# A two-layer mLSTM/SSD trunk on one core: decay distances from plain fp32 tiles, built ahead, and another order in the mixer's first group

## The chip, the cores and the metric

The kernel runs on one core of a Trainium2 chip. The metric is the time of one execution on the device in microseconds (us), as the median over several runs. PE is TensorE (PEld its weight loads), DVE is VectorE, ACT is ScalarE, POOL is GpSimd and SP is SyncE, which issues the weight transfers.

## What is computed

Two layers (DEPTH 2) on 256 tokens (SEQ) of width 1024, all in fp32. Each layer is a half-step SwiGLU FFN (hidden 2816), the mixer, a second half-step FFN and a gated per-layer embedding. The mixer is what matters here: one projection feeds an mLSTM with 4 heads and a Mamba-2 SSD with 32 heads in 4 groups. Both work in chunks of 128 tokens, so there are NC = 2 chunks.

```
proj = rmsnorm(h) @ w_in            # q, k, v, o_pre, i_pre, f_pre, z, xbc, dt_raw, gate_pre
dt   = softplus(dt_raw + dt_bias);  dA = dt * a_neg;  acs = cumsum(dA) in a chunk
decay[t,s] = exp(acs[t] - acs[s]) for s <= t, else 0        # per head
y_intra = (C_t . B_s) * decay[t,s] @ (x * dt)
y_inter = (C_t . state at the chunk's start) * exp(acs[t])  # only chunk 1 has a state
ha = mlstm(q, k, v, i, f);  yb = rmsnorm((y_intra + y_inter + x*d_skip) * silu(z))
h  = h + (sigmoid(g_a) * (ha @ w_a) + sigmoid(g_b) * (yb @ w_b)) @ w_out
```

The "distances" of the title are the sums acs[t] - acs[s], one 128x128 tile per head and chunk.

## The kernel before

**Split products.** A large product runs as three matmuls in fp32r, a reduced form of fp32: each fp32 operand is split in a high part and a rest (w_hi and w_lo, u_hi and u_lo), and hi·hi, lo·hi and hi·lo are added up in a bank of PSUM. Weights pass through a ring of three slots. SP loads w_raw, ACT copies it to w_hi (L483), DVE subtracts for w_lo (L768), and PE takes it. The sizes of one slot are 1024 rows by 256 columns, and one slot is a **unit**: 48 matmuls of 256 columns.

**Mixer.** A layer's mixer has four groups (body(0, True), then a loop over the other three). A group has nine units in the order BC (B and C of the SSD), QK, X01 and X23 (its x), V, Z0, Z1, O and GA. Their results go in turn to banks 0, 1 and 2 (unit p to bank p % 3), from which DVE reads them (evac, L968). Between the units stand the small products of the group, in plain fp32 or fp32r, in banks 3 to 7. Each engine's order is written out by hand, and semaphores tie the engines together: step(p) in ACT and DVE prepares the weights of unit p+2.

**Distances before.** The sum from s to t is a product with a triangular matrix of ones: segments (L1452 to L1466) multiplies tri_gt_r with R, where R[s',t] is dA[s'] for s' <= t. The work goes by quarters b of a group's 8 heads, in each chunk c. POOL builds R for two heads twice, from dA_hi and dA_lo (L426), into two buffers in turn, PE makes two matmuls of 256 columns of them, and after every quarter POOL may refill its buffer (seg_done, r_built). In chunk 1 PE also multiplies R with ones_r, which gives acs[t] itself, into banks 4 and 5. ACT takes the exp of a half (four heads) from the banks (L586 for the tiles, L594 for acs[t] into cs). The one bank of a distance is 4 + 2c + half.

**First group.** It also prepares the gates for all groups. small (L1416) projects 40 columns, softplus_gates on DVE makes dA (L912) and its two parts (L916, L918). gates (L1429 to L1433) multiplies dA for w_end and transposes the mLSTM's gate inputs to 4 rows, gate_rows on DVE (L924 to L946) runs the running sums and maxima over them and ends with M4 (L946), and gates_back (L1439) turns them back into columns (tokc, tok_ready). scores (L1481, L1482) needs M4.

**Last part of a group.** chunk heads of the mLSTM (L1519 to L1521), transposes of x (L1527), memory read (L1532), state (L1537), outputs in two parts (L1547, L1549), and the transposes of the normalised mLSTM rows (L1554). After the groups come four gate units (K_GB, banks q % 3), a column sum with its row scale rB (L703 on ACT), and a merge loop that starts in bank 0.

## Time and profile before

| | us |
|---|---|
| median of 3 runs | 1681.77 |
| lowest and highest run | 1680.89, 1685.76 |
| the profiled execution | 1680.02 |
| its span, first to last instruction | 1678.3 |
| PE busy | 1612.6 (96%) |
| DVE busy | 1050.1 (63%) |
| ACT busy | 729.3 (43%) |
| POOL busy | 264.3 (16%) |

The span is what the views of the trace measure, and the profiled execution's own time is 1.72 us above it. Matmuls are pipelined: one counts as busy for 0.28 us while the next starts 0.12 us after it, so the time that a matmul takes from PE is read from start to start. An idle time in the views is what stands between the end of one instruction and the start of the next on an engine, with the instruction that ended it.

### The profile page before, as it was taken

How to read it: one execution, taken by the hardware profiler on the slowest of the kernel's cores; microseconds unless marked ns; L12 is line 12 of the kernel's file. 1: busy time of each engine (PE TensorE's matmuls, PEld its weight loads, DVE VectorE, ACT ScalarE, POOL GpSimd, SP SyncE). 2: the span in 40 equal slices, each digit the busy share in tenths (PEclk: the TensorE clock that was granted, in tenths of full speed). 3: DMA queues.
4: the chain of work that ended last, by engine and by line, in shares of the span. 5: the costliest groups of instructions: out<-in, count | busy, mean ns of one | idle time of the engine just before them, and what ended most of it. 6: DMA issues, size and time to landing. Idle time of an engine off the chain costs nothing.

```text
span 1678.3 us, 24971 instructions
## 1 busy us (share of the span) xinstructions
PE 1612.6 (96%) x9888; PEld 1422.0 (85%) x9888; DVE 1050.1 (63%) x1288; ACT 729.3 (43%) x880; POOL 264.3 (16%) x272
## 2 busy tenths in 40 slices
PE   7999989999999999999999999899999999999997
PEld 5888788998999978888778888798999999788885
DVE  5544587777886645454665455877787765454445
ACT  5444434344345435343554444344344443544444
POOL 0000024455430000000000000355435300000000
PEclk9999989999999999999999999899999999999999
DMA  7555534454544555555555554254453455465551
GB/s 240 194 176 196 153 105 125 123 149 127 152 148 161 169 178 201 184 187 179 165 187 177 189 186 138 89 156 121 150 150 100 150 186 189 156 203 179 196 175 63
DMA packets 245236, 270.85 MB, mean 161 GB/s; under 512 B 12504, under 2 KB 226360, under 8 KB 245176
## 3 DMA queue, kind: packets, MB, share of 16 engines
q1 hardware_dynamic: 239472, 266.90, 49.5%
q10 hardware_dynamic: 5704, 3.13, 0.7%
q8 instruction: 40, 0.66, 0.2%
q14 instruction: 20, 0.16, 0.0%
HBM read 268.94 MB, written 1.05 MB: 161 GB/s over the span
## 4 chain that ended last, share of the span: by engine, by line
PE 83%; DVE 6%; issue 5%; POOL 3%; ACT 2%; DMA 0%; POOLq 0%; DVEq 0%; SPq 0%; ACTq 0%
PE bank L1291 26%; PE bank L1317 16%; PE bank L1319 16%; PE bank L1318 16%; DVE w_lo L768 2%; POOL R L426 2%; PE bank L1359 1%; PE bank L1465 1%; PE bank L1303 1%; PE bank L1304 1%; PE bank L1305 1%; PE bank L1635 1%; PE bank L1312 1%; PE bank L1547 1%; ACT w_hi L483 1%
## 5 line engine op out<-in xcount | busy, mean ns | idle before, releaser
L768 DVE TENSOR_TENSOR w_lo<-w_raw,w_hi 128x2048 fp32r<-128x2048 f32 x252 | 590.6, 2345 | 306.4 <-ACT w_hi L483 306.2
L483 ACT ACTIVATE w_hi<-w_raw 128x2048 fp32r<-128x2048 f32 x252 | 481.6, 1913 | 232.2 <-PE bank L1319 119.9
L1291 PE MATMUL bank<-u_hi,w_hi 128*128 128x256 f32 x1152 | 336.0, 292 | 2.5 <-DVE u_lo L803 2.5
L1291 PE MATMUL bank<-u_lo,w_hi 128*128 128x256 f32 x1152 | 331.0, 287 | 0.0
L1291 PE MATMUL bank<-u_hi,w_lo 128*128 128x256 f32 x1152 | 330.8, 287 | 0.0
L1291 PEld LDWEIGHTS bank<-u_hi,w_hi 128*128 128x128 f32 x1152 | 226.4, 197 | 7.4 <-issue 6.3
L1291 PEld LDWEIGHTS bank<-u_lo,w_hi 128*128 128x128 f32 x1152 | 226.5, 197 | 0.1
L1291 PEld LDWEIGHTS bank<-u_hi,w_lo 128*128 128x128 f32 x1152 | 226.2, 196 | 0.0
L398 POOL TENSOR_TENSOR rms<-var,m_half 128x2 f32<-128x2 f32 x11 | 7.7, 698 | 1084.3 <-DVE var L796 1071.1
L1317 PE MATMUL bank<-w_hi,u_hi 128*128 128x512 f32 x416 | 166.3, 400 | 5.9 <-DVE u_lo L803 4.3
L1317 PE MATMUL bank<-w_hi,ha_hi 128*128 128x512 f32 x416 | 164.9, 396 | 3.5 <-DVE w_lo L768 3.5
L1319 PE MATMUL bank<-w_hi,u_lo 128*128 128x512 f32 x416 | 162.9, 392 | 0.0
L1318 PE MATMUL bank<-w_lo,u_hi 128*128 128x512 f32 x416 | 162.5, 391 | 0.0
L1319 PE MATMUL bank<-w_hi,ha_lo 128*128 128x512 f32 x416 | 162.4, 390 | 0.0
L1318 PE MATMUL bank<-w_lo,ha_hi 128*128 128x512 f32 x416 | 162.0, 389 | 0.0
L1317 PE MATMUL bank<-w_hi,h_hi 128*128 128x512 f32 x352 | 140.0, 398 | 0.4
L1319 PE MATMUL bank<-w_hi,h_lo 128*128 128x512 f32 x352 | 139.2, 396 | 0.0
L1318 PE MATMUL bank<-w_lo,h_hi 128*128 128x512 f32 x352 | 139.1, 395 | 0.0
L537 ACT ACTIVATE h_hi<-bank 128x512 fp32r<-128x512 f32 x44 | 26.3, 598 | 165.4 <-PE bank L1359 165.4
L1317 PEld LDWEIGHTS bank<-w_hi,u_hi 128*128 128x128 f32 x416 | 78.5, 189 | 22.5 <-DVE w_lo L768 6.4
L1317 PEld LDWEIGHTS bank<-w_hi,ha_hi 128*128 128x128 f32 x416 | 78.1, 188 | 21.0 <-DVE w_lo L768 5.3
L1319 PEld LDWEIGHTS bank<-w_hi,u_lo 128*128 128x128 f32 x416 | 78.4, 188 | 16.8
(259 smaller groups left out, 2579.9 us busy)
## 6 DMA issues: line engine op xcount, KB each, us to landing
w_raw<-in_w_ffn_dram SPq DMA_DIRECT2D x264, 512.0 KB, 4.3
w_raw<-in_w_in_dram SPq DMA_DIRECT2D x160, 512.0 KB, 4.6
w_raw<-in_w_branch_b_dram SPq DMA_DIRECT2D x32, 512.0 KB, 3.9
w_raw<-in_w_branch_a_dram SPq DMA_DIRECT2D x16, 512.0 KB, 4.0
w_raw<-in_w_out_dram SPq DMA_DIRECT2D x16, 512.0 KB, 4.2
w_raw<-in_w_ple_gate_dram SPq DMA_DIRECT2D x16, 512.0 KB, 4.2
y_feat<-in_w_ple_dram ACTq DMA_DIRECT2D x2, 1024.0 KB, 4.9
h<-in_x_dram SPq DMA_DIRECT2D x2, 512.0 KB, 4.9
```

What stands on the lines that cost most here:

```text
L426: i = g_.tensor_tensor(R[:, b % 2, q, :, :], tri_le[:, :].unsqueeze(1).broadcast_to([P, 2, P]), part[:, c, bass.ds(g * EH + 2 * b, 2)].bit ...
L483: a_.activation(whi[slot][:, :, :], raw[slot][:, :, :], ACT.Copy).then_inc(sem["w_hi"], 1)
L537: a_.activation(h1_hi[b][:, :, :], two(6 - 2 * b), ACT.Copy).then_inc(sem["h1_hi_ready"], 1)
L768: v_.tensor_tensor(wlo[slot][:, :, :], raw[slot][:, :, :], whi[slot][:, :, :].bitcast(F32), ALU.subtract).then_inc(sem["w_lo"], 1)
L1291: i = mm(o, w[slot][:, k, cs], x[:, k, :], start=(k + q == 0 and not seeded), stop=(k == KD - 1 and q == 2 and not seeded), skip_group_che ...
L1303: mm(o, xh[:, k, cs], whi[slot][:, k, :], start=(k == 0), stop=False)
L1304: mm(o, xh[:, k, cs], wlo[slot][:, k, :], start=False, stop=False)
L1305: i = mm(o, xl[:, k, cs], whi[slot][:, k, :], start=False, stop=(k == KD - 1))
L1312: ins = nc.tensor.transpose(bank[b][:, chunk(t)], h[:, c, (4 * q + t) * P:(4 * q + t + 1) * P], ident[:, :])
L1317: mm(o, xh, wh, start=start, stop=False, skip_group_check=True)
L1318: mm(o, xh, wl, start=False, stop=False, skip_group_check=True)
L1319: return mm(o, xl, wh, start=False, stop=stop, skip_group_check=True)
```

## The change

Distances: R is now plain fp32 and holds four heads for one chunk (128x512). POOL builds it with one multiplication from dA instead of four of 256 columns. The two R tiles lie in the storage of xwe and zth, which the group uses later. The products use tri_gt and ones in plain fp32, one matmul of 512 columns per tile: four tiles a group for the distances (seg_done counts to 6 a group instead of 8), and two (from_start, banks 6 and 7) for acs[t], read from the same R. The two tiles of chunk 0 are built by POOL in the group before (at its end, ahead of the ysum addition). dA_hi and dA_lo are gone.

Order: in the later groups each distance tile stands half a unit or more away from the one before, and from_start lies in the middle of V. In the first group gates moves from the last quarter of X23 to ahead of X23, gates_back and scores move into the middle of V, from_start lies in Z0, and the chunk's last products move one unit back. cb no longer waits for the exp of acs[t]. M4 has 128 rows, cleared by POOL once a layer. The gate units after the groups use banks 0, 1, 0, 2, and the merge loop waits for their evacuation instead of for rB. chunk_heads, inputs_transposed, memory_read, state and outputs are the same code as before, now as functions (their waits are the same but that the transposes also wait for the exp of acs[t], since both use banks 6 and 7).

```diff
+    GATE_BANK = (0, 1, 0, 2)
...
-        M4 = sb("M4", [MH, MH, S])
+        M4 = sb("M4", [P, MH, S])
...
-        R, _ = at("R", [P, 2, 2, 2, P], F32R, a)
...
+        R = (xwe[:, :].rearrange("p (e t) -> p e t", e=4),
+             zth[:, :, :].rearrange("p a b -> p (a b)").rearrange("p (e t) -> p e t", e=4))
...
+            def distances_of(g, c, half):
+                g_.tensor_tensor(R[half][:, :, :], tri_le[:, :].unsqueeze(1).broadcast_to([P, 4, P]),
+                                 dA[:, c, bass.ds(g * EH + 4 * half, 4)].unsqueeze(2).broadcast_to([P, 4, P]),
+                                 ALU.mult).then_inc(sem["r_built"], 1)
...
+                def token_columns():
+                    pool.wait_ge(sem["tok_ready"], lay * 2 + 2)
+                    g_.tensor_copy(gtk[:, :].unsqueeze(2), tokc[:, :, bass.ds(g, 1)]).then_inc(sem["gtk_ready"], 1)
+                if first:
+                    pool.wait_ge(sem["dA_ready"], lay + 1)
+                    for half in range(2):
+                        distances_of(g, 0, half)
+                else:
+                    token_columns()
+                for half in range(2):
+                    pool.wait_ge(sem["seg_done"], G * 6 + (half + 1))
+                    distances_of(g, 1, half)
+                if first:
+                    token_columns()
...
+                if not last:
+                    pool.wait_ge(sem["yi_done"], G + 1)
+                    pool.wait_ge(sem["zth_ready"], G * 2 + 2)
+                    for half in range(2):
+                        distances_of(g + 1, 0, half)
...
+                g_.memset(M4[:, :, :], 0.0).then_inc(sem["m4_clear"], 1)
+                group(lay, 0, True, False)
+                with nc.gpsimd.Fori(1, NG - 1) as g:
+                    group(lay, g, False, False)
+                group(lay, NG - 1, False, True)
...
-                            act.wait_ge(sem["seg_done"], G * 8 + 10)
-                            a_.activation(cs[:, 4 * b:4 * b + 4, :], bank[4 + b][:, :].rearrange("p (e t) -> p e t", e=4),
+                            act.wait_ge(sem["seg_done"], G * 6 + (5 + b))
+                            a_.activation(cs[:, 4 * b:4 * b + 4, :], bank[6 + b][:, :].rearrange("p (e t) -> p e t", e=4),
...
                     step(2)
-                    if not first:
-                        decay(0)
-                    step(3)
                     if first:
+                        step(3)
                         act.wait_ge(sem["cum_done"], lay + 1)
                         a_.activation(w_end[:, :], bank[7][:, 0:SH], ACT.Exp).then_inc(sem["cum_exp"], 1)
+                        step(4)
                         decay(0)
                         act.wait_ge(sem["row_back"], lay + 1)
...
                         tanh_conv(1, xcv[:, 0:2, :])
+                        score_exp()
+                        step(5)
+                        decay(1)
+                        transposed_copies()
+                        decay_from_start()
+                        tanh_conv(2, xcv[:, 2:4, :])
                     else:
+                        decay(0)
+                        step(3)
                         tanh_conv(1, xcv[:, 0:2, :])
                         score_exp()
                         decay(1)
+                        step(4)
                         decay_from_start()
-                    step(4)
-                    if first:
-                        score_exp()
-                    tanh_conv(2, xcv[:, 2:4, :])
-                    if first:
-                        decay(1)
-                        decay_from_start()
...
-                    step(5)
+                        tanh_conv(2, xcv[:, 2:4, :])
+                        transposed_copies()
+                        step(5)
...
-                ch.add(v_.tensor_copy(dA_hi[:, :, :], dA[:, :, :]))
-                ch.wait()
-                v_.tensor_tensor(dA_lo[:, :, :], dA[:, :, :], dA_hi[:, :, :].bitcast(F32), ALU.subtract)\
-                    .then_inc(sem["dA_ready"], 1)
+                v_.scalar_tensor_tensor(out=dA[:, :, :], in0=spx[:, :, 4:36], scalar=-1.0,
+                                        in1=e_a[:, :].unsqueeze(1).broadcast_to([P, NC, SH]),
+                                        op0=ALU.mult, op1=ALU.mult).then_inc(sem["dA_ready"], 1)
...
                     conv(1, 1, (2, 3), xcv[:, 0:2, :])
                     silu(1, xcv[:, 0:2, :])
-                    if not first:
+                    if first:
+                        distances()
+                    else:
                         weigh_scores()
-                    else:
-                        distances()
                     evac(X23, xin[:, 0, :, 3:])
+                    if first:
+                        values()
+                        step(4)
+                        weigh_scores()
+                        mask_cb()
                     taken(X23)
                     conv(2, 0, (4, 5), xcv[:, 2:4, :])
...
+                    if not first:
+                        values()
                     silu(2, xcv[:, 2:4, :])
-                    if first:
-                        weigh_scores()
-                    mask_cb()
-                    step(4)
+                    if not first:
+                        mask_cb()
+                        step(4)
                     dve.wait_ge(sem["ysum_ready"], G + 1)
                     evac(Z0, zs[:, 0:2, :])
                     step(5)
...
+                    if not first:
+                        weighted_inputs()
                     dve.wait_ge(sem["z_tanh"], G * 2 + 1)
                     v_.scalar_tensor_tensor(out=zs[:, 0:2, :], in0=zth[:, :, :], scalar=1.0, in1=zs[:, 0:2, :],
                                             op0=ALU.add, op1=ALU.mult).then_inc(sem["zth_ready"], 1)
                     step(6)
                     evac(Z1, zs[:, 2:4, :])
+                    if first:
+                        weighted_inputs()
...
-                        for b in (2 * half, 2 * half + 1):
-                            pe.wait_ge(sem["r_built"], G * 8 + (4 * c + b + 1))
-                            todo = [(4 + 2 * c + half, tri_gt_r)]
-                            if c == 1:
-                                pe.wait_ge(sem["exp_done"], G * 4 + (half + 1))
-                                todo.append((4 + half, ones_r))
-                            for bk, w in todo:
-                                for q in range(2):
-                                    i = mm(bank[bk][:, (b % 2) * S:(b % 2 + 1) * S], w[:, :],
-                                           R[:, b % 2, q, :, :], start=(q == 0), stop=(q == 1))
-                            i.then_inc(sem["seg_done"], 1)
+                        pe.wait_ge(sem["r_built"], G * 4 + (2 * c + half + 1))
+                        mm(bank[4 + 2 * c + half][:, :], tri_gt[:, :], R[half][:, :, :], start=True, stop=True)\
+                            .then_inc(sem["seg_done"], 1)
+                    def from_start():
+                        for half in range(2):
+                            pe.wait_ge(sem["exp_done"], G * 4 + (3 + half))
+                            mm(bank[6 + half][:, :], ones[:, :], R[half][:, :, :], start=True, stop=True)\
+                                .then_inc(sem["seg_done"], 1)
                     def cb():
                         pe.wait_ge(sem["cv_ready"], G * 3 + 1)
-                        pe.wait_ge(sem["acs_exp"], G * 2 + 2)
+                        pe.wait_ge(sem["exp_done"], G * 4 + 2)
...
                         unit(QK, lambda *a: feat(*a, between=lambda: norm_rows(lay, 1)))
                         small_back(lay)
                         unit(X01, feat)
-                        unit(X23, lambda *a: feat(*a, between=lambda: gates(lay)))
+                        gates(lay)
+                        unit(X23, feat)
                         segments(0, 0)
-                        gates_back(lay)
                         segments(0, 1)
-                        scores()
+                        def rows_and_scores():
+                            gates_back(lay)
+                            scores()
+                        unit(V, lambda *a: tok(*a, between=rows_and_scores))
                         pe.wait_ge(sem["tok_ready"], lay * 2 + 2)
-                        unit(V, lambda *a: tok(*a, between=lambda: segments(1, 0)))
+                        segments(1, 0)
                         segments(1, 1)
                         cb()
+                        unit(Z0, lambda *a: feat(*a, between=from_start))
+                        chunk_heads()
+                        unit(Z1, feat)
+                        inputs_transposed()
+                        memory_read()
+                        unit(O, feat)
+                        state()
+                        outputs(0)
+                        outputs(1).then_inc(sem["y_done"], 1)
                     else:
                         unit(BC, feat)
-                        unit(QK, feat)
-                        segments(0, 0)
-                        unit(X01, lambda *a: feat(*a, between=lambda: segments(0, 1)))
-                        segments(1, 0)
+                        unit(QK, lambda *a: feat(*a, between=lambda: segments(0, 0)))
+                        segments(0, 1)
+                        unit(X01, lambda *a: feat(*a, between=lambda: segments(1, 0)))
+                        segments(1, 1)
                         evac(QK)
                         scores()
-                        unit(X23, lambda *a: feat(*a, between=lambda: segments(1, 1)))
-                        unit(V, tok)
+                        unit(X23, feat)
+                        unit(V, lambda *a: tok(*a, between=from_start))
                         cb()
-                    unit(Z0, feat)
...
+                        unit(Z0, feat)
+                        chunk_heads()
+                        inputs_transposed()
+                        unit(Z1, feat)
+                        memory_read()
+                        state()
+                        outputs(0)
+                        unit(O, feat)
+                        outputs(1).then_inc(sem["y_done"], 1)
...
-                    feat((K_GB + q) % RING, q % 3, u_hi, u_lo)
+                    pe.wait_ge(sem["evac"], lay * NE + (NG * GU + (q + 1 if q != 2 else RING + 1)))
+                    feat((K_GB + q) % RING, GATE_BANK[q], u_hi, u_lo)
                     if q == 0:
...
-                    pe.wait_ge(sem["yB_ready"], lay + 1)
+                    pe.wait_ge(sem["evac"], lay * NE + (NG * GU + RING + 3))
```

**PE, first group, around the gates.** w_hi_54 is the slot of X01, w_hi_52 that of X23. Before:

```order
L1291 MATMUL bank<-u_hi,w_hi_52 128x256
L1291 MATMUL bank<-u_lo,w_hi_52 128x256
L1291 MATMUL bank<-u_hi,w_lo_55 128x256
L1429 MATMUL bank<-dA,tri_gt 128x32
L1432 MATMUL bank<-ident,pre 4x128
L1433 MATMUL bank<-ident,spx 4x128
L1432 MATMUL bank<-ident,pre 4x128
L1433 MATMUL bank<-ident,spx 4x128
L1291 MATMUL bank<-u_hi,w_hi_52 128x256
L1291 MATMUL bank<-u_lo,w_hi_52 128x256
```

After:

```order
L1316 MATMUL bank<-u_hi,w_hi_54 128x256
L1316 MATMUL bank<-u_lo,w_hi_54 128x256
L1316 MATMUL bank<-u_hi,w_lo_57 128x256
L1454 MATMUL bank<-dA,tri_gt 128x32
L1457 MATMUL bank<-ident,pre 4x128
L1458 MATMUL bank<-ident,spx 4x128
L1457 MATMUL bank<-ident,pre 4x128
L1458 MATMUL bank<-ident,spx 4x128
L1316 MATMUL bank<-u_hi,w_hi_52 128x256
L1316 MATMUL bank<-u_lo,w_hi_52 128x256
```

The gates stood inside X23 and stand ahead of it now, 36 matmuls earlier.

**PE, later groups, from X01 to the scores.** REGISTER_ALU and ISA rows are waits' bookkeeping. Before:

```order
L1465 MATMUL bank<-R,tri_gt_r 128x256 x2
L1465 MATMUL bank<-R,ones_r 128x256 x2
L1458 REGISTER_ALU
L1465 MATMUL bank<-R,tri_gt_r 128x256 x2
L1465 MATMUL bank<-R,ones_r 128x256 x2
L1452 REGISTER_ALU
L1481 MATMUL bank<-qT,kT 128x128 x2
L1482 ISA
L1482 MATMUL bank<-M_89,ones 128x256
```

After:

```order
L1316 MATMUL bank<-u_hi,w_hi_54 128x256
L1316 MATMUL bank<-u_lo,w_hi_54 128x256
L1316 MATMUL bank<-u_hi,w_lo_57 128x256
L1481 REGISTER_ALU
L1482 MATMUL bank<-zth,tri_gt 128x512
L1477 REGISTER_ALU
L1503 MATMUL bank<-qT,kT 128x128 x2
L1504 ISA
L1504 MATMUL bank<-M_82,ones 128x256
```

Eight matmuls in two waited-for steps (half 0 of chunk 1) stood here; one plain fp32 tile (half 1 of chunk 1) does now, and half 0 lies in X01.

**POOL, end of a group.** Before:

```order
L442 TENSOR_TENSOR seg<-seg,cbm 128x1024
L445 REGISTER_ALU
L446 TENSOR_TENSOR cs<-cs,bcv 128x1024
L398 TENSOR_TENSOR hrms<-hvar,m_half 128x2
L451 TENSOR_TENSOR ysum<-ysum,zs 128x1024
```

After:

```order
L444 TENSOR_TENSOR seg<-seg,cbm 128x1024
L447 REGISTER_ALU
L448 TENSOR_TENSOR cs<-cs,bcv 128x1024
L397 TENSOR_TENSOR hrms<-hvar,m_half 128x2
L404 ISA
L404 TENSOR_TENSOR xwe<-tri_le,dA 128x512
L404 ISA
L404 TENSOR_TENSOR zth<-tri_le,dA 128x512
L458 TENSOR_TENSOR ysum<-ysum,zs 128x1024
```

The next group's two tiles of chunk 0 now stand between hrms and ysum.

## Rows read from the trace of the kernel before

**Rows 1.** The page: busy us, share of the span and instructions of each engine.

```profile
PE 1612.6 (96%) x9888; PEld 1422.0 (85%) x9888; DVE 1050.1 (63%) x1288; ACT 729.3 (43%) x880; POOL 264.3 (16%) x272
```

**Rows 2.** Waits of PE in the whole span: us in total, times, longest.

```profile
PE bank L1465 <- POOL R L426: 14.0, 12, 2.0
PE bank L1439 <- DVE M L946: 8.3, 2, 4.2
...
PE bank L1465 <- ACT seg L586: 3.8, 6, 1.7
PE bank L1474 <- ACT cs L594: 3.7, 2, 2.0
PE bank L1291 <- ACT rB L703: 3.1, 2, 1.6
```

**Rows 3.** Stretches of PE: length, busy (instructions), granted clock, DMA share, GB/s.

```profile
227.76:289.71 61.95, 54.03 (x414) 0.89 0.37 103
1052.22:1114.63 62.41, 54.60 (x413) 0.89 0.36 109
289.71:494.00 204.29, 197.64 (x1618) 0.97 0.49 138
1114.63:1321.72 207.09, 199.61 (x1617) 0.97 0.44 137
428.30:494.00 65.70, 64.01 (x542) 1.00 0.50 142
```

**Rows 4.** Timeline of PE, a quarter pair's distances: start, us, engine, line, operation.

```profile
450.44 0.64 PE L1465 MATMUL bank<-R,tri_gt_r 128*128 128x256 f32 x4
450.91 0.27 PE L1291 MATMUL bank<-u_hi,w_hi 128*128 128x256 f32 x1
```

**Rows 5.** Timeline of PE, plain fp32 products and the unit behind them.

```profile
349.05 0.59 PE L1532 MATMUL bank<-cst,qT 128*128 128x257 f32 x2
349.48 1.02 PE L1537 MATMUL bank<-xwe,btok 128*128 128x512 f32 x2
350.43 1.09 PE L1547 MATMUL bank<-seg,xw 128*64 128x128 f32 x16
351.46 0.39 PE L1291 MATMUL bank<-u_hi,w_hi 128*128 128x256 f32 x1
351.68 0.28 PE L1291 MATMUL bank<-u_lo,w_hi 128*128 128x256 f32 x1
```

**Rows 6.** Timeline of PE, first group of layer 0: X01, gates, gates_back.

```profile
227.76 0.39 PE L1291 MATMUL bank<-u_hi,w_hi 128*128 128x256 f32 x1
...
238.09 0.41 PE L1429 MATMUL bank<-dA,tri_gt 128*128 128x32 f32 x2
...
247.41 2.72 PE L1439 MATMUL bank<-ident,r_x 4*128 4x4 f32 x12 [4.08 <-DVE M L946]
```

**Rows 7.** Timeline of DVE, first group of layer 0: dA, and the gate rows.

```profile
237.32 0.23 DVE L912 SCALAR_TENSOR_TENSOR dA<-spx,e_a 128x64 f32<-128x64 f32 x1
...
246.15 1.20 DVE L946 TENSOR_TENSOR M<-r_m,ident 4x1024 f32<-4x1024 f32 x1
```

**Rows 8.** Timeline of all engines, the same group's mLSTM norm.

```profile
283.85 0.42 ACT L660 ACTIVATE pm<-num 128x256 f32<-128x256 f32 x1 [1.22 <-DVE num L1090]
...
286.36 0.62 DVE L1110 TENSOR_SCALAR num<-num,hsc 128x256 f32<-128x256 f32 x2
```

**Rows 9.** Timeline of all engines, second group: X23's start, the chain beside it.

```profile
320.05 0.58 PE L1291 MATMUL bank<-u_hi,w_hi 128*128 128x256 f32 x1
...
320.23 0.61 DVE L1009 TENSOR_SCALAR pm<-bank,gtk 128x128 f32<-128x128 f32 x2 [3.35 <-PE bank L1482]
...
328.05 1.07 ACT L586 ACTIVATE seg<-bank 128x512 f32<-128x512 f32 x2
```

**Rows 10.** Timeline of POOL, second group, building R.

```profile
314.69 2.66 POOL L426 TENSOR_TENSOR R<-tri_le,dA_lo 128x256 fp32r<-128x256 f32 x1
317.31 0.61 POOL L426 TENSOR_TENSOR R<-tri_le,dA_hi 128x256 fp32r<-128x256 f32 x1
```

210 lines of the change are left out of this document (96 added, 114 removed).

## The prediction

> **What bounds the kernel now.** The page comes first: PE is busy 96% of the span, DVE 63%, and no other engine is near that [rows 1]. So the time is PE's work plus PE's idle time, and next one reads who PE waits for. The waits view of PE over the span names five causes that touch the lines of this change: R from POOL 14.0 us, M4 from DVE 8.3, the exp of seg 3.8, the exp of cs 3.7 and rB 3.1, together 32.9 us, all in the mixer [rows 2]. The third view cuts PE's time into stretches and gives the granted clock of each. Both first groups (from the start of X01 to the start of GA) have a clock of 0.89 and all later groups of a layer together 0.97, but the last group of layer 0 alone 1.00: 65.70 us with 64.01 busy [rows 3]. That last row is the measure for all: a later group is 64.0 us of work at the full level of 2.4 GHz. What stands above it in the others is idle time and time at the half level of 1.2 GHz, in which a unit's matmuls need twice the time. The six later groups take 204.29 + 207.09 = 411.4 us, 27.4 above 6 x 64.0 [rows 3]; 14.1 of these are idle (411.38 less 197.64 and 199.61 busy), 13.3 the clock.
>
> **The change, part by part.**
>
> *Plain fp32 tiles, PE's price.* Before, a tile of four heads is four fp32r matmuls of 256 columns, 0.47 us from start to start [rows 4]; six tiles a group are 2.8 us. No row has a plain fp32 matmul with R, so its price is bounded. A plain product of 257 columns holds PE 0.43 us (349.05 to 349.48), which is 0.86 for 512; the product of 512 columns takes 0.95 until the next starts [rows 5]. I take 0.86, since the tiles are of the same shape as the first scaled up and have no narrow output behind them, and keep 0.95 as the upper end. Behind plain products the first matmul of a unit holds 0.22 instead of 0.12 (351.46 to 351.68) [rows 5]; I put as much on the way in, 0.2 for each place where plain work newly interrupts a unit. A later group has four such places (in QK, behind it, in X01, in V; the fourth tile joins the scores, which are plain already): 6 x 0.86 + 0.8 - 2.8 = 3.2, taken as 3.1; the ends are 2.4 (no cost of switching) and 3.7. A first group has one new place: +2.6. So PE gets 6 x 3.1 + 2 x 2.6 = 23.8 us more work. This is the debit side, and it is most of what the waits offer.
>
> The Trainium skill speaks against this part: "FP8 and Floating Point Precision", section TensorE Precision Notes, says that true fp32 needs four passes through the array. Four passes of 512 columns at 2.4 GHz would be 0.853 us, an estimate from that page, and by it the tiles alone cost 48 x (0.853 - 0.47) = 18.4 us.
>
> *R built by one multiplication, chunk 0 a group ahead.* POOL takes 0.61 us for 256 columns undisturbed and 2.66 when it falls together with a DVE operation [rows 10], so a tile of 512 costs 1.2 us, or about 3.3 when disturbed. Half of each pair is now built while the mLSTM norm or output work runs, 18 us before PE needs it; the other half is built after the first tiles (three quarters through QK, and behind it) and needed three quarters through X01, 5.8 us or 48 x 0.12 later, and behind X01. Both fit, even disturbed. The eight matmuls that waited in two steps on the exp of seg and on a refilled R are gone, since the ones product is a step of its own in V. So the 14.0 and the 3.8 us go. POOL's two builds ahead stand before ysum, which waits for ACT's square anyway; they may push one w_lo of DVE by 2 us, and the unit it serves starts 10 us later.
>
> *What is late next in a later group.* from_start, in the middle of V, waits for the exp of chunk 1's seg. The row of before gives both sides from X23's start at 320.05: PE needs a unit (5.76) and half of V (2.88), 8.64 us; DVE's distances start 0.18 behind it, and the first of ACT's two exps starts at 328.05 and ends about 0.55 later, at 8.55 [rows 9]. The slack is nil. I take 0.2 us a group, ends 0 and 1.0. A later group is then 64.0 + 3.1 + 0.2 = 67.3 us at full clock, six are 403.8, against 411.4: **-7.6 us**. With no idle time over 1 us I expect no half clock there: the one later group that kept 1.00 had a single idle time of 1.69 [rows 3], and the R waits elsewhere reach 2.0 [rows 2].
>
> *First group.* Idle before is 61.95 - 54.03 = 7.9 us [rows 3], 4.08 of it at gates_back [rows 6]. Gone with the new order: gates_back stands half of V after the tiles, at about 249, and DVE's gate rows end at 247.35 [rows 7]; the two R waits (POOL starts on dA and has all of X23) and the cs wait at cb. New: gates stands ahead of X23. X01 starts at 227.76 and needs 5.8 us, so PE is there at 233.6; before it came at 238.09 [rows 6]. But dA, which gates multiplies, is only ready at 237.55 [rows 7]. dA_hi and dA_lo come behind dA, so their loss does not bring it forward. That is **4.0 us idle**, at a place that had none. Everything behind it on PE, X23 first, waits too. Second, state now comes one unit later but the last products follow at once: ACT squares the mLSTM rows only behind the copy of the state, and from that square's start to the end of num on DVE it is 283.85 to 286.98, 3.1 us [rows 8], plus 0.6 for the copy; both parts of outputs fill 2.9 us of it. 0.9 us idle. Clock: before, 0.11 x 61.95 is 6.8 us lost, that is 13.6 us at half, 4.1 of them idle, so 4.8 us of real loss. After, one idle time of 4.0 instead of four; I take half the time at half clock, a loss of 3.0, ends 1.5 and 6.8. Sum: +2.6 work, -7.9 + 4.9 idle, -4.8 + 3.0 clock = -2.2 each, **-4.4 us**.
>
> *Merge.* Bank 0 is free earlier, since the last gate unit writes bank 2, so PE need not wait for rB: **-3.1 us** [rows 2]. DVE alone needs rB, a unit and two more later. *Small.* M4's clearing (one POOL memset a layer of 1024 columns, some 1 us) falls ahead of the group's constants while DVE still works on the row scale; 0, at worst 1 us a layer. M4's product keeps its columns: 0.
>
> **Sum.** -7.6 - 4.4 - 3.1 = -15.1 us. On the profiled execution, 1680.02, that is 1664.9. The median of the runs lies 1.75 above that execution: **1667 us** against 1681.77, 0.9% less.
>
> **The rivals.**
>
> 1. *No new stall at the gates or no drop behind it.* If dA came earlier than 237.55, 4.0 + 3.0 would go twice: 1653. I see no reason in the rows for dA to move; only the clock may stay up, 6 us: 1661.
>
> 2. *The clock stays as it was.* The plain tiles do not mend the half level: 13.3 us in the later groups and 3.8 more in the first ones come back, -15.1 + 17.1 = +2: 1684, no change to be measured. For it speaks that a 4.0 us gap is in each first group as before; against it that the later groups have no gap of that kind left.
>
> 3. *Slower: from_start becomes the new wait.* Its slack is nil [rows 9]. If DVE's chain ahead of it slips, by one collision with POOL (2.66 against 0.61, 2 us [rows 10]), PE idles 2 us in V and falls to half for some 3.5 us, 1.7 lost: 3.7 x 6 = 22 us, and the result is 1689. It decides the sign from 15.1 / 6 = 2.5 us a group. Against it: in that stretch POOL has nothing queued between the R tiles and pm, which comes behind the exp.
>
> 4. *A part only.* The fp32 tiles cost their upper end (3.7) and from_start 1.0: +1.4 x 6 = 8 us: 1675.
>
> **Chances and range.** A difference of 0.3% (5 us) is about what a measurement of this kernel can tell from none. Forecast (1661 to 1671) 0.53; rival 1 0.12; rival 4 0.17; rival 2 0.10; rival 3 0.08. The range leaves out rival 3, most of rival 2 and the far part of rival 1: 1658 to 1679. Faster by over 0.3% (below 1676.7): 0.53 + 0.12 + most of rival 4 = 0.79; within: the rest of 4 and rival 2, 0.13; slower (above 1686.8) 0.08.
>
> **What would show it.** In the profile after, the waits view should have no R line from POOL beyond 1 us in total, no M4 wait, no rB wait, and a new wait of PE for dA, twice, 4.0 us each. The four-heads tile should hold PE 0.86 to 0.95 us. Each later group should be 67 to 68 us with a clock of 1.00, each first group about 59.8 from X01 to GA. A wait for seg at the ones product above 0.5 us a group speaks for rival 3, a clock under 0.98 in later groups for rival 2. The forecast is wrong if the stall at the gates is not there, if a plain tile costs over 1.1 us, or if idle times come up at places that the rows of before don't show, for instance weights (w_lo) in the first group, where DVE's order is rearranged.

## The result: 36.6 us faster, more than twice the forecast

| | before | after |
|---|---|---|
| median of 4 runs, us | 1681.67 | 1645.11 |
| lowest and highest | 1680.89, 1685.76 | 1644.43, 1645.88 |
| span of the profiled execution | 1678.3 | 1644.1 |

The ratio is 0.9772 (95% interval 0.9755 to 0.9788). The forecast was 1667 with a range of 1658 to 1679; the time lies 13 us below its lower end. The sign was right, the size was not.

The page after: PE is busy for 11.4 us less than in [rows 1] (the time at half clock counts as busy too), although the plain fp32 tiles were to cost it 23.8 more.

```profile
PE 1601.2 (97%) x9792; PEld 1399.9 (85%) x9792; DVE 1047.4 (64%) x1282; ACT 730.1 (44%) x880; POOL 205.4 (12%) x178
```

The waits of PE after (us in total, times, longest). None of the five of [rows 2] is left. dA, num and cst are new; the first two are nearly what the prediction said, twice 4.0 and twice 0.9. This view lists no wait for seg at from_start; a small one hides there all the same (see "M4 with 4 rows again").

```profile
PE bank L1454 <- DVE dA L931: 7.6, 2, 3.8
...
PE bank L1605 <- DVE num L1138: 1.7, 2, 0.9
...
PE bank L1527 <- ACT cst L667: 0.5, 2, 0.2
```

Stretches of PE after (length, busy, granted clock, DMA share, GB/s). The first four answer to [rows 3]: the two first groups, then the later groups of each layer. The last two are the end of layer 0's groups up to the merge loop, and what follows up to the end of the second FFN (merge, output projection, FFN), which the change leaves alone but for the merge loop's first wait.

```profile
226.05:284.58 58.53, 53.61 (x402) 0.94 0.41 112
1036.64:1093.96 57.32, 52.40 (x401) 0.97 0.38 111
284.58:482.14 197.56, 197.56 (x1581) 1.00 0.51 145
1093.96:1291.54 197.58, 197.58 (x1582) 1.00 0.47 144
482.14:513.10 30.96, 30.96 (x255) 1.00 0.38 122
...
513.10:816.30 303.20, 301.34 (x1631) 1.00 0.56 183
```

The same untouched stretch in the kernel before took 2.2 us more, with no other idle time and no other clock:

```profile
526.76:832.16 305.40, 303.53 (x1628) 1.00 0.54 180
```

The later groups have no idle time in this view and the full clock: 65.85 us each. Set beside the forecast, in us of the span (1678.3 to 1644.1):

| stretch | forecast | measured |
|---|---|---|
| six later groups | -7.6 | -16.2 |
| two first groups | -4.4 | -8.5 |
| to the merge loop, both layers | -3.1 | -3.6 |
| stages that the change leaves alone | 0 | -5.6 |
| the stretch ahead of X01, both layers | 0 | -0.3 |
| sum | -15.1 | -34.2 |

The last row but one is the clock ahead of the mixer: layer 0 has no half clock there after (-2.1 and +0.4), layer 1 has one (+1.4). No run ties it to the change.

### The profile page after: what moved, and what is told of

Read it like the earlier page. It is cut to its first block, busy times and chain, and to the rows that moved or that the text cites. A ratio compares the mean times of both kernels' runs of the same rounds, so it can differ in the third digit from the quotient of the medians.

```text
span 1644.1 us, 24426 instructions
## 1 busy us (share of the span) xinstructions
PE 1601.2 (97%) x9792; PEld 1399.9 (85%) x9792; DVE 1047.4 (64%) x1282; ACT 730.1 (44%) x880; POOL 205.4 (12%) x178
## 4 chain that ended last, share of the span: by engine, by line
PE 90%; DVE 5%; ACT 2%; issue 2%; DMA 0%; POOL 0%; SPq 0%; POOLq 0%; DVEq 0%; ACTq 0%
PE bank L1316 31%; PE bank L1342 16%; PE bank L1343 16%; PE bank L1344 16%; PE bank L1482 1%; DVE w_lo L787 1%; PE bank L1384 1%; PE bank L1330 1%; PE bank L1329 1%; PE bank L1328 1%; PE bank L1686 1%; ACT w_hi L499 1%; DVE xcv L997 1%; PE bank L1544 1%; PE bank L1488 1%
## 5 line engine op out<-in xcount | busy, mean ns | idle before, releaser
L1316 PE MATMUL bank<-u_hi,w_hi 128*128 128x256 f32 x1152 | 341.7, 297 | 2.5 <-DVE u_lo L822 2.5
L1316 PEld LDWEIGHTS bank<-u_hi,w_hi 128*128 128x128 f32 x1152 | 223.1, 194 | 9.3 <-issue 7.8
```

The source lines that it names most:

```text
L1316: i = mm(o, w[slot][:, k, cs], x[:, k, :], start=(k + q == 0 and not seeded), stop=(k == KD - 1 and q == 2 and not seeded), skip_group_che ...
```

## The experiments

The ratio in each compares with runs of the kernel before on the same chip, whose median there was 1681.8 to 1683.7. Line numbers are those of each kernel's own code.

### Where the operands lie: the stages that were not touched

The gain of 5.6 us in untouched stages needed a cause first. From start to start the merge matmuls with yb took 116.7 ns before and 113.5 after (mean of 752), the FFN matmuls with h1 233.1 and 229.0 (1030); those with u and ha did not move. yb and h1 are exactly the tiles that lie in the shared stage storage, and this begins 2400 bytes lower after the change, since tri_gt_r, ones_r, dA_hi, dA_lo and three sp tiles left the room below it.

```diff
+        top[0] += 32
         base = top[0]
         a = base
```

> The changed kernel with 32 bytes left free in front of all tiles that share the stage storage (h1_hi, h1_lo, yb_hi, yb_lo among them); nothing else is changed. In the changed kernel that storage begins 2400 bytes lower than before, at a multiple of 64 bytes instead of a multiple of 32 alone; here it begins at a multiple of 32 alone again, at nearly the same place. Theory alignment: this sets the spacing of the matmuls that read these tiles; the merge matmuls with yb go from 113.5 ns back to 116.7 and the FFN matmuls with h1 from 229.0 to 233.1, and the kernel takes about 5.2 us more (2.2 + 2.2 + 1.2 less 0.4, the gains in the stages that the change does not touch): 1650. Rival distance: what counts is the place 2400 bytes lower, or it is something else than the place: spacings stay at 113.5 and 229.0 and the time at 1645.

> The kernel before with the same 32 bytes, so that its stage storage begins at a multiple of 64 bytes, 2432 bytes above that of the changed kernel. Theory alignment: spacings fall from 116.7 to 113.5 ns (yb) and from 233.1 to 229.0 (h1), and the time falls by about 5.2 us: 1676.5. Rival distance: nothing moves, 1681.7.

Measured: e1 1652.75 us (ratio 0.9818, 0.9797 to 0.9840), yb 118.3 ns, h1 233.2. e2 1683.49 us (ratio 1.000, 0.9987 to 1.0013), yb 117.8, h1 233.4. Thirty-two bytes cost the changed kernel some 7 us, so the place is the cause. But e2's storage begins at a multiple of 64 and gained nothing: the theory of alignment fell. One loop of the merge, 96 matmuls with yb, in the kernel after, in e1 and in e2:

```profile
535.85:546.93 11.08, 11.08 (x99) 1.00 0.58 189
```

```profile
536.93:548.47 11.54, 11.54 (x98) 1.00 0.57 184
```

```profile
552.25:563.74 11.49, 11.49 (x99) 1.00 0.56 185
```

The next run puts the storage of the kernel before at the very byte where the changed kernel has it:

```diff
-        tri_gt_r = sb("tri_gt_r", [P, P], F32R)
-        ones_r = sb("ones_r", [P, P], F32R)
...
-        top_all = max(a, a2, a3, a4, a5)
+        a6 = max(a, a2, a3, a4, a5)
+        tri_gt_r, a6 = at("tri_gt_r", [P, P], F32R, a6)
...
+        top_all = a6
```

> The kernel before with tri_gt_r, ones_r, sp_a, sp_b, sp_c, dA_hi and dA_lo (2400 bytes a partition) moved behind everything else, so that the shared stage storage begins at the very byte where it begins in the changed kernel; nothing else is changed. Theory placement: the changed kernel's gain in stages that it does not touch comes from that place alone. Shifting by 32 bytes took 7 us from the changed kernel and gave the kernel before nothing, so it is the exact place and not its alignment alone: h1 matmuls go from 233.1 to 229.0 ns, yb from 116.7 to 113.5, time -5.2 us (2.2 + 2.2 + 1.2 - 0.4). Rival: the spacings come with the new code in another way: no change.

Measured: 1676.12 us, ratio 0.9955 (0.9937 to 0.9973), 5.7 us less than the median of the kernel before beside it (1681.82; the interval allows 4.5 to 10.6). yb 113.5, h1 229.0, to the tenth what the changed kernel has. So the 5.6 us that the forecast lacked come from the place.

What in the address counts? Three kernels put five operands at other distances from the weight slots; the lines shown are those of the second for u and yb:

```diff
+        def skip(off, residue):
+            while (off - origin) % 512 != residue:
+                off += 32
+            return off
+
+        origin = top[0]
         raw = [sb(f"w_raw{i}", [P, KD, NP]) for i in range(RING)]
...
+        top[0] = skip(top[0], 192)
         u_hi = sb("u_hi", [P, KD, S], F32R)
...
-        a2 = base
+        a2 = skip(base, 0)
```

> The changed kernel with five operands at other places, all by the distance of their first byte from that of the weight slots, modulo 512: u 64 (0 in both kernels), ha 128 (0), yb 256 (192 in the changed kernel), h1 buffer 0 256 and buffer 1 320 (192); the computation is the same. So far, for products whose moving operand has 256 columns, that distance and the spacing were: 0 (ha) 120.1 ns, 32 (yb, before) 116.7, 64 (yb) 117.8, 192 (yb, after) 113.5, 224 (yb) 118.3. Theory distance modulo 512: the spacing follows that number whichever tile it is, so u at 64 falls from 120 to 117.8, and that alone is 3456 x 2.3 ns = 8 us of the kernel. Rival: each tile has its own spacing by its absolute place or its role: u stays at 120.

> The same with u 192, ha 256, yb 0, h1 buffer 0 at 0 and buffer 1 at 128. Theory distance modulo 512: u at 192 takes the 113.5 ns of yb, 3456 matmuls x 6.6 ns = 23 us less, its products of 512 columns go from 227.6 to 229.0 (3 us more), and yb at 0 takes the 120.1 of ha (768 x 6.6 = 5 us more), h1 at 0 the 227.6 of u: about 1630. Rival (own spacing of each tile): u stays at 120 and the time within 5 us of 1645.

> The same with u 320, ha 384, yb 128, h1 buffer 0 at 384 and buffer 1 at 448. No distance among these has been measured. Theory distance modulo 512: what ha shows at 128 in the first of these kernels, yb shows here. Rival: they differ by over 1 ns.

Measured: e9 1655.25 us (one run), e10 1639.96 (ratio 0.9743, 0.9718 to 0.9769), e11 1653.98 (one run). The mean spacings from start to start, each over several hundred matmuls, by the distance modulo 256:

| distance | moving operand, 256 columns | stationary operand, 512 columns moved |
|---|---|---|
| 0 | u 119.8, ha 119.6, ha 120.0, yb 119.9 | u 227.6, ha 227.7, h1 227.1 |
| 32 | yb 116.7 | h1 233.1 |
| 64 | yb 117.8, u 117.4, u 117.5 | h1 233.4, u 233.3, u 233.3 |
| 128 | ha 118.7, yb 118.6, ha 118.6 | ha 232.6, ha 232.8 |
| 192 | yb 113.5, u 114.9 | h1 229.1, u 229.1 |
| 224 | yb 118.3 | h1 233.2 |

Different tiles at the same distance agree within 0.6 ns, except u at 192, which has 1.4 more than yb. Places 256 apart agree too. So the theory of e9 holds for the spacings, with a period of 256, and the two roles of the table want different places: the moving operand 192, the stationary one under 512 columns 0. A third role does not follow the table's second column. In V, u is the stationary operand and 256 columns of weights are moved (some 350 matmuls): 119.8 ns at 0, 114.6 and 114.1 at 64 (e9, e11), 115.6 at 192 (e10). There 0 is the worst of the places tried. From GA to the quarter of QK, 132 matmuls with u, in the kernel after and in e10:

```profile
350.42:366.34 15.92, 15.92 (x136) 1.00 0.33 80
```

```profile
349.47:364.53 15.06, 15.06 (x135) 1.00 0.26 73
...
530.60:542.30 11.70, 11.70 (x100) 1.00 0.57 183
```

u won 0.86 us in this stretch, and yb, put at 0 (the second row), lost 0.62 a loop. e9 and e11 were slow because u and ha as stationary operands went from 227.6 to 233, and yb from 113.5 to 119.9 and 118.6. For e10's time 1630 was expected and 1640 came: u took 114.9 ns and not 113.5, 4.6 us over 3267 matmuls, and PE, now faster, waited longer, for seg at from_start above all (2.3 us in the waits view).

In all these kernels the weight slots stood still, so distance and plain address were the same thing. One more run moved everything, the slots too:

```diff
+        top[0] += 64
         raw = [sb(f"w_raw{i}", [P, KD, NP]) for i in range(RING)]
```

> The changed kernel with every tile 64 bytes higher, the weight slots among them; all distances between tiles stay. Theory distance: the spacing of two operands' products is set by where they lie to each other, so nothing moves: u 119.8 ns, yb 113.5, h1 229.1, time 1645. Rival, plain address modulo 256: yb takes what it had at the next place 64 bytes up (119.9), u what it had at 64 (117.4), and the stationary u of 512 columns goes from 227.6 to 233: u alone 8 us less, yb and the stationary operands some 5 and 12 us more, about 1655, as the kernel with u at 64 had (1655.3).

Measured: 1644.83 us (one run); u 119.8, yb 113.5, h1 229.1. Nothing moved:

```profile
349.40:365.32 15.92, 15.92 (x135) 1.00 0.31 81
534.81:545.89 11.08, 11.08 (x98) 1.00 0.57 189
```

So the plain address falls, and what counts is where an operand lies to something that moved with it. That this is the weight slots is likely, since each of these products reads one, but no run moved the slots alone. Whether the operand meets PE's own weight loads or the writes of ACT, DVE and the DMAs into the slots stays open too: no run separates them.

Does placement help a kernel whose mixer waits? The kernel before, with u at 192, yb and h1 at 192 and ha at 0, by moving small tiles only:

```diff
+        dcol = sb("dcol", [P, SI // P])
+        w_end = sb("w_end", [P, SH])
         u_hi = sb("u_hi", [P, KD, S], F32R)
...
+        gcb = sb("gcb", [P, 6])
+        gdk = sb("gdk", [P, 4])
         ha_hi = sb("ha_hi", [P, 2 * MH, S], F32R)
```

> The kernel before with small tiles moved to other places and nothing else: the 2400 bytes behind everything as in the run with the low base, dcol and w_end ahead of u_hi and gcb and gdk ahead of ha_hi, so that u lies 192 bytes from a multiple of 256 (from the weight slots), ha at 0, yb and h1 at 192. Theory: the gain of the place is independent of the change: 5.6 us as with the low base, and of u's 3200 matmuls x 4.9 ns = 16 us less 1155 x 1.5 ns = 1.7 the part that waits do not eat; in the changed kernel a later group gained 1.65, the stretch to the merge loop 1.56 a layer, so at least 6 x 1.65 + 2 x 1.56 = 13 less 1.7: 1682 - 5.6 - 11 = 1665. Rival: PE's waits in the mixer of before (R, M4, seg, cs) take it back: 1671 to 1676.

Measured: 1670.61 us, ratio 0.9935 (0.9921 to 0.9948): 11.4 us less, of which the low base gives 5.7. The rival holds, at the edge of its 1671 to 1676. The later groups took 205.18 and 203.67 us against 204.29 and 207.09 in [rows 3], with 9 us idle in each layer where there were 6.7 and 7.5: PE is faster in its units and waits longer for R, 19.4 us instead of 14.0.

```profile
287.83:493.01 205.18, 196.22 (x1617) 0.96 0.48 138
1111.44:1315.11 203.67, 194.66 (x1617) 0.97 0.46 139
```

```profile
PE bank L1466 <- POOL R L427: 19.4, 16, 2.3
```

### The price of a plain fp32 tile

```diff
+                        mm(bank[4 + 2 * c + half][:, :], tri_gt[:, :], R[half][:, :, :], start=True, stop=True)
                         mm(bank[4 + 2 * c + half][:, :], tri_gt[:, :], R[half][:, :, :], start=True, stop=True)\
                             .then_inc(sem["seg_done"], 1)
```

> The changed kernel with every distance tile of segments issued twice into the same bank: four plain fp32 matmuls of 512 columns more a group, 32 in all. Theory: the tile costs PE 0.86 us and interrupting a unit of fp32r matmuls costs nothing on top; a later group goes from 65.85 to 69.3 us (+3.4) and the kernel's six later groups take +20.6; in the first groups the four tiles stand in an engine order where PE waits anyway, +0 to +6.9 for both. 1666 to 1673. Rival (the prediction's price, with 0.2 for each place where plain work interrupts a unit inside the present group): a second copy behind the first costs 0.86 and the present tile 1.06, so that the group would have to show 0.2 more at the first copy than at the second. Second rival, the upper end of 0.95 a tile: 69.65 a later group.

Measured: 1671.02 us, ratio 0.9931 (0.9913 to 0.9949). The later groups of a layer take 207.93, 69.31 each, against 65.85. Four more tiles are 3.45 us, so 0.863 a tile.

```profile
285.91:493.84 207.93, 207.93 (x1606) 1.00 0.48 137
```

The timeline of the same kernel at the quarter of QK (start, us, engine, line, operation; x2 because one plain product of 512 columns is recorded as two matmuls), where L1482 is the first copy and L1483 the second:

```profile
301.70 0.28 PE L1316 MATMUL bank<-u_hi,w_lo 128*128 128x256 f32 x1
301.83 1.02 PE L1482 MATMUL bank<-xwe,tri_gt 128*128 128x512 f32 x2
302.69 1.02 PE L1483 MATMUL bank<-xwe,tri_gt 128*128 128x512 f32 x2
303.14 0.68 PE L1316 MATMUL bank<-u_hi,w_hi 128*128 128x256 f32 x1
303.66 0.28 PE L1316 MATMUL bank<-u_lo,w_hi 128*128 128x256 f32 x1
```

The copy behind the unit holds PE 0.86, and from the second copy to the unit's second matmul there are 0.97, which is 0.86 and the usual 0.12. Interrupting a unit with such a tile costs nothing. The theory holds; both rivals fall. The unit's first matmul behind a tile starts early and lasts long: its work has moved up into the tile's time and is not lost. Whether this is so for the 0.22 of [rows 5], which stands behind smaller products, no run separates. True fp32 as four passes of 512 columns at 2.4 GHz, an estimate of 0.853 us from the Trainium skill ("FP8 and Floating Point Precision", TensorE Precision Notes), agrees with the 0.863 measured.

### M4 with 4 rows again

```diff
-                        mm(bank[3][:, S:2 * S], ones[:, :], M4[:, bass.ds(g, 1), :].rearrange("p a b -> p (a b)"),
+                        mm(bank[3][:, S:2 * S], ones[0:MH, :], M4[0:MH, bass.ds(g, 1), :].rearrange("p a b -> p (a b)"),
```

> The changed kernel with M4's product on 4 rows again (ones and M4 cut to 4 partitions) instead of 128. Theory: a product with 4 rows among full ones costs PE 0.3 to 0.4 us more a group (1.39 us from the scores to the unit's second matmul before, 1.00 after), eight groups: +2.4 to +3.1 us, 1648. Rival: that difference came from elsewhere (the waited-for exp, fp32r products ahead of it): no change, 1645.

Measured: 1648.56 us, ratio 0.9791 (0.9769 to 0.9814). From the scores to the second matmul behind them 1.38 us instead of 1.00; a later group takes 66.04 instead of 65.85. So the 128 rows gave 0.38 us at the place but 0.19 in the length of a group, 1.1 us in six of them. The rest of the difference in time is mostly layer 1's first group, whose clock was lower (60.44 us at 0.92 against 57.32 at 0.97), so that the time hit its forecast in part by luck.

The other 0.19 stands at from_start. In the changed kernel its two products start 0.86 us apart in the first group, where seg is long ready, and 0.97 apart in a later group:

```profile
261.67 1.02 PE L1488 MATMUL bank<-xwe,ones 128*128 128x512 f32 x2
262.53 1.02 PE L1488 MATMUL bank<-zth,ones 128*128 128x512 f32 x2
...
386.53 1.13 PE L1488 MATMUL bank<-xwe,ones 128*128 128x512 f32 x2
387.50 1.02 PE L1488 MATMUL bank<-zth,ones 128*128 128x512 f32 x2
```

The first of them also starts 0.20 behind the unit's matmul and not 0.12. Together that is a wait for seg of 0.18 us in each of the six later groups, too short for the idle column, since a matmul counts as busy for 0.28. In e4 PE comes there 0.38 later, both steps are 0.12 and 0.86 in all later groups, and the wait is gone.

The scores and the unit behind them, in the kernel with M4 on 4 rows, and then in the changed kernel:

```profile
376.61 0.61 PE L1503 MATMUL bank<-qT,kT 128*128 128x128 f32 x4
377.14 0.69 PE L1504 MATMUL bank<-M,ones 4*128 x2
377.76 0.39 PE L1316 MATMUL bank<-u_hi,w_hi 128*128 128x256 f32 x1
377.99 0.28 PE L1316 MATMUL bank<-u_lo,w_hi 128*128 128x256 f32 x1
```

```profile
376.94 0.61 PE L1503 MATMUL bank<-qT,kT 128*128 128x128 f32 x4
...
377.94 0.28 PE L1316 MATMUL bank<-u_lo,w_hi 128*128 128x256 f32 x1
```

### The banks of the gate units alone

The kernel before with GATE_BANK (0, 1, 0, 2) and the merge loop's wait on the evacuation instead of rB.

> The kernel before with one part of the change alone: the four gate units use banks 0, 1, 0, 2 and the merge loop waits for their evacuation instead of for rB. Theory: the stretch from GA of the last group to the merge loop goes from 32.76 to 30.96 us in each layer as it did with the whole change, -3.6 us in all, 0.5 more than the wait of 3.1 that the prediction counted; everything else stays. Rival: the stretch became shorter with the rest of the change (the last group ends otherwise, POOL's ysum): -3.1 or less.

Measured: 1680.30 us, ratio 0.9986 (0.9976 to 0.9996). The stretch to the merge loop is 30.97 us in both layers, as expected and as with the whole change:

```profile
493.99:524.96 30.97, 30.97 (x255) 1.00 0.39 126
1323.05:1354.02 30.97, 30.97 (x255) 1.00 0.37 122
```

So -3.6 us there, 0.5 more than the wait of [rows 2]. In the whole time less of it is seen, since layer 1's first group took 64.10 us instead of 62.41, with a clock of 0.87.

### Building ahead, taken back

POOL builds the tiles of chunk 0 at the start of their own group:

```diff
-                if not last:
-                    pool.wait_ge(sem["yi_done"], G + 1)
-                    pool.wait_ge(sem["zth_ready"], G * 2 + 2)
-                    for half in range(2):
-                        distances_of(g + 1, 0, half)
...
                 else:
+                    for half in range(2):
+                        distances_of(g, 0, half)
                     token_columns()
```

> The changed kernel without the building ahead: POOL builds the two tiles of chunk 0 at the start of their own group, behind the group's constants, instead of at the end of the group before. Theory: it is the building ahead that lets the later groups run without idle time. In the second group POOL is through with the constants at 301.4 and PE is at the first tile at 300.5, so the tile comes at 302.4 undisturbed (1.04 us) or at 304.5 beside a DVE operation (3.1): 2 to 4 us idle a later group, and half clock behind it (1.5 to 3 more, as the later groups of the kernel before stand at 65.7, 68.5 or 70.0 us): 66.9 + 2 to 4 + 1.5 = 68 to 72 a group, 1658 to 1680. Rival: the four tiles instead of eight quarters and their spread are what counts, and the tile comes in time: 1645 to 1650.

Measured: 1647.04 us (one run), 1.9 more than the changed kernel. The rival holds. Only the second group of each layer is longer (67.4 against 65.9), PE waits 1.3 us for the tile there; in the third and fourth groups it comes in time.

```profile
PE bank L1478 <- POOL xwe L404: 2.6, 2, 1.3
```

The building ahead is worth 1.5 us in the second group of each layer, about 3 in all. The rest of the idle time went out of the later groups without it. That this is because a chunk needs two tiles instead of four refilled pairs, with half a unit or more of PE's work between two tiles, fits the rows but is not shown: no run takes the number and the order of the tiles apart.

### The first group: the stall at gates

The kernel with gates in X23 again, then the same with POOL's products kept away from a convolution, and last this edit without moving gates:

```diff
-                        gates(lay)
-                        unit(X23, feat)
+                        unit(X23, lambda *a: feat(*a, between=lambda: gates(lay)))
```

> The changed kernel with one move undone: in the first group gates stands after three quarters of X23 again instead of ahead of it. Theory: the two idle times of 3.8 us at gates and the half clock behind them come from that move alone. dA is ready at 235.8 in both; X23 would start at 232.1, so PE is at gates at 236.4 and does not wait. X23 then takes 5.8 us instead of 8.0 and PE is 6.0 us earlier in layer 0 (3.8 + 2.2) and 5.5 in layer 1 (3.8 + half of 3.4). Against it stands a new wait at gates_back in V: the gate rows end at about 244.1 as now, PE is there at 242.9: 1.2 us each. Together 9 us less: 1636. Rival: the gate rows are the true bound (DVE's chain after them sets what comes later, X01's evacuation and the first exps), so that waits of the same 3.8 us come up further on: 1642 to 1645.

Measured: 1647.19 us, ratio 0.9783 (0.9761 to 0.9804), nothing gained. The waits for dA are gone, and others stand in their place, these two the largest:

```profile
PE bank L1527 <- ACT cst L667: 4.3, 2, 2.2
...
PE bank L1464 <- DVE M L961: 3.0, 2, 1.5
```

The first groups are as long as with the stall (the rival), at a clock of 0.97:

```profile
226.20:285.45 59.25, 52.91 (x402) 0.97 0.41 113
1037.53:1095.30 57.77, 52.78 (x401) 0.97 0.38 110
```

cst is late because ACT waits for DVE's evacuation of Z0, and this stands behind the third convolution. In the changed kernel DVE's two rows of it take 2.82 and 6.69 us, while POOL multiplies seg:

```profile
258.83 2.82 DVE L994 TENSOR_SCALAR xcv<-xin,gcw,gcb 128x256 f32<-128x256 f32 x2
261.69 6.69 DVE L997 SCALAR_TENSOR_TENSOR xcv<-xin,gcw,xcv 128x256 f32<-128x256 f32 x6
```

```profile
259.00 4.87 POOL L444 TENSOR_TENSOR seg<-seg,cbm 128x1024 f32<-128x1024 f32 x2 [4.48 <-DVE cbm L1030]
264.27 2.51 POOL L448 TENSOR_TENSOR cs<-cs,bcv 128x1024 f32<-128x1024 f32 x1 [0.40 <-ACT cs L610]
```

```diff
+                if first:
+                    pool.wait_ge(sem["conv_done"], G * 3 + 3)
                 pool.wait_ge(sem["cbm_done"], G + 1)
```

> The changed kernel with gates back inside X23 and, in the first group alone, one wait more on POOL: its seg multiplications begin when DVE's third convolution is through. Theory from the run with gates in X23 alone, which took away both stalls at gates and gained nothing (1647.2): in the first group DVE is the bound, and its third convolution takes 9.7 us (2.8 + 6.9) instead of 3.4 because it stands beside POOL's two multiplications of 1024 columns; PE waits 1.1 us for xcv and 2.2 for cst behind it. With the two apart DVE is about 6 us earlier at the evacuation of Z0, these waits go, and the half clock after them: 3.3 to 5 us a layer, 1637 to 1641. Rival: POOL's products come too late then (m_ready, cs_ready) or DVE's next operations, the weights, take the collision instead: 1644 to 1648.

Measured: 1641.75 us, ratio 0.9760 (0.9744 to 0.9776). The convolution takes 3.5 us instead of 9.5, the waits for cst and xcv are gone (that for num grew from 0.9 to 1.7 a layer), and both first groups are 56.47:

```profile
257.78 0.73 DVE L996 TENSOR_SCALAR xcv<-xin,gcw,gcb 128x256 f32<-128x256 f32 x2
258.54 2.71 DVE L999 SCALAR_TENSOR_TENSOR xcv<-xin,gcw,xcv 128x256 f32<-128x256 f32 x6
```

In the changed kernel three of the convolution's eight instructions take 2.5 us where each takes 0.4 to 0.5 alone, and the first of the three ends at 261.65, 0.15 behind POOL's product. That fits what the Trainium skill says in "SBUF — State Buffer", section SBUF: two separate sides: DVE and GpSimd share a pair of ports that one of them holds for a whole instruction.

> The changed kernel with POOL's seg products behind the third convolution in the first group, and gates left ahead of X23 where the change put it. Theory: DVE is the bound of the first group once gates is there; the stall of 3.8 us at gates delays X23 but DVE's chain, which begins with dA, not: as with gates in X23 (1641.8), within 2 us. Rival (the prediction's step): now that the collision is gone, the stall at gates and the half clock behind it are on the path and cost 3 to 6 us a layer: 1648 or more.

Measured: 1644.33 us, ratio 0.9777 (0.9762 to 0.9792), between the two. From X01 to GA, in layer 0 and layer 1:

| | gates ahead of X23 | gates in X23 |
|---|---|---|
| POOL beside the convolution | 58.53, 57.32 | 59.25, 57.77 |
| POOL behind it | 58.14, 57.95 | 56.47, 56.47 |

As whole kernels the four took 1645.11 (nothing), 1647.19 (gates in X23), 1644.33 (POOL behind) and 1641.75 us (both). Neither edit alone gains clearly, both together do: 2.1 and 0.9 us in the groups, 3.4 in the median, with all of its runs below all runs of the changed kernel. Single cells of the table hold the clock of one execution: the upper left is at 0.94 and 0.97, the lower left at 0.94 twice, the right column at 0.97, and e4 and e12, which have this part as in the upper left, show 57.57 and 60.44, and 57.17 and 57.29. Two chains of nearly equal length end in this group, PE's with the stall at gates and DVE's with the convolution. The theory (stall hidden) and the rival (stall on the path) are each half right: the stall is as late as the thing that would come next.

### A version that beats both

gates in X23, POOL behind the convolution, u and yb at 192, ha and h1 at 0:

> The changed kernel with gates in X23, POOL's seg products behind the third convolution in the first group, and operands placed by what the runs showed (distance from the weight slots modulo 256): u 192 and yb 192, which are mostly the moving operand, ha 0 and h1 0, which are mostly the stationary one. Theory placement by residue: yb at 113.5 ns as in the changed kernel (119.9 at 0: 768 x 6.4 ns = 4.9 us less than the kernel with u 192, ha 256 and yb 0, which took 1640.0), h1 at 227.6 instead of 229.7 (2.2 us less), and 3.4 us less from the first groups, as that edit gave alone: 1640 - 4.9 - 2.2 - 3.4 = 1629.5. Rival: the terms don't add up, since PE comes faster to DVE's first group and waits there, 1633 or more.

Measured: 1629.69 us, ratio 0.9694 (0.9681 to 0.9707), 15.4 us less than the changed kernel and what the sum of single terms (1629.5) said. u 114.9 ns, yb 113.5, h1 227.1.

```profile
226.24:282.75 56.51, 51.77 (x402) 0.97 0.42 114
1027.54:1084.06 56.52, 50.16 (x402) 1.00 0.39 114
282.75:475.69 192.94, 191.81 (x1582) 1.00 0.52 149
```

The later groups are 64.3 and 64.5 us now. They idle for 1.1 us a layer: PE's units have become so fast that the wait for seg at from_start, 0.18 us a group in the changed kernel, shows in the waits view (seg, 2.3 us in all).

## Why the prediction was wrong, step by step

**The bound, the waits and what they leave: right.** PE was the bound. R, M4, seg, cs and rB left the waits view. The later groups kept the full clock, as forecast, here and in every kernel built on the changed one. Rival 2 did not come, nor rival 3: PE reaches from_start a little before seg is ready and waits 0.18 us in each later group, where the prediction took 0.2 from a slack of nil.

**PE's price of the tiles: the term that was mis-sized most.** The tile was put at 0.86 and measured 0.863 (e5). The step that failed is the 0.2 us for each of four places where plain work interrupts a unit: they are 0. M4's product was said to keep its price because it keeps its columns; on 128 rows it costs 0.38 us less (e4). And the fp32r work that went was 2.95 us in the last group of layer 0 (24 matmuls, start to start), not 2.8. So a later group got 6 x 0.863 - 2.95 - 0.38 = 1.85 us more work instead of 3.1.

The measured length agrees: 65.85 - 64.0 = 1.85. Two small waits cancel in it. The 64.0 of [rows 3] hold 0.15 us of waiting, since the group's idle time of 1.69 moved PE's next start by 1.84 (452.22 to 454.18 in the timeline of before, less the usual 0.12); and the changed kernel waits 0.18 at from_start. So the group was forecast at 67.3 and took 65.85, and six times 1.45 is the 8.6 that the later groups missed, up to rounding. The lower bound that the prediction wrote for this term (2.4, no cost of switching) was nearly the truth. The reading that failed was of [rows 5]: the longer gap behind plain products was taken for a price of every switch, though the row ahead of it has to be read with it. The timeline of the changed kernel shows the whole of it, 0.98 us from the tile to the unit's second matmul:

```profile
300.48 1.02 PE L1482 MATMUL bank<-xwe,tri_gt 128*128 128x512 f32 x2
300.94 0.68 PE L1316 MATMUL bank<-u_hi,w_hi 128*128 128x256 f32 x1
301.46 0.28 PE L1316 MATMUL bank<-u_lo,w_hi 128*128 128x256 f32 x1
```

**First groups: the idle times right, the rest too high.** Idle after is 58.53 - 53.61 = 4.92 us and 57.32 - 52.40 = 4.92; forecast 4.9. The clock took 1.7 us from layer 1 (0.03 x 57.32) and some 3.0 from layer 0 (3.5 by its 0.94, less the part in which PE stood idle anyway); forecast 3.0. What is left is work at full clock, 50.6 and 50.7 us. Before, by the prediction's own way (61.95 - 7.9 - 4.8, and 62.41 - 7.8 - 4.8), it was 49.2 and 49.8, so it rose by 1.4 and 0.9 and not by 2.6. The errors of 0.2, 0.38 and 0.15 above make 0.7 of that in each layer; the rest was not traced. With layer 1's clock these are the 4.1 us of the table.

The prediction treated the stall at gates as a pure loss of 4.0 and its clock. e3, e15 and e8 show it is not: without it, other waits of about the same length come up, until DVE's chain is shortened as well. For the change's own time that made no difference. But rival 1 (1661, or 1653 without the stall) was priced from PE alone. e3 removed the stall and gained nothing; it did so by moving gates, and no run has an earlier dA.

**Merge: right, 3.6 instead of 3.1** (e7).

**Stages left alone: the step that was missing.** The prediction had no term for them. The diff takes 2400 bytes out below the shared storage, in plain sight, but nothing in the profile of before hinted that an address has a price. Even had it been known, the direction would not have followed without a table like the one above. It is 5.6 of the 19.1 us, and e6 gives the same gain to the kernel before.

8.6 (later groups), 4.1 (first groups), 0.5 (merge), 5.6 (placement) and 0.3 (clock ahead of X01) make the 19.1 us between -15.1 and -34.2.

**The range.** It was made from bounds of each term taken one at a time. The errors had the same sign, and a switching price that does not exist stood in the middle of the debit. With the lower bound of the tiles' price the sum would have been 6 x 0.7 + 2 x 0.2 = 4.6 us lower, 1662, still 17 above the measured time: the rest is placement, M4, the price of the fp32r tiles, and work and clock in the first groups. So the sign was right for the reasons given (the five waits went), and the size was not.

## What to carry to other kernels

Read a gap behind an operation together with the start of that operation: a matmul that starts early and lasts long has moved its work, not added to it. Waits of a few tenths of a microsecond on PE are not in the idle column, here 0.18 a group; spacings from start to start show them. If removing a stall is to be priced, follow the engine that ends it to its next appointment; here the chain of the other engine was nearly as long. And when tiles are added or removed, ask what moves behind them in SBUF: after any such edit compare the start-to-start spacing of matmuls in stages that were not edited.
